# Opening phase in token pieces, sample tile joined for two column blocks, scores of the samples in four column groups

## What is computed

```
h = rmsnorm(x, norm_g)
z = h @ w_in                                   # (tokens, 4096) @ (4096, 9728)
u_a, gate_a, glu_val, glu_gate, gate_b, q, gate_c = split(z)
o_a = pool_mix(u_a) * silu(gate_a)             # windowed means 2/4/8/16 minus token, group map, scale
a   = glu_val * sigmoid(glu_gate)
o_b = (silu(layernorm(depthwise_conv31(a))) @ w_pw) * silu(gate_b)
o_c = softmax(q @ mem_k.T / 16) @ mem_v * silu(gate_c)    # 4 heads, 256 memory tokens
y   = rmsnorm(x + concat(o_a, o_b, o_c) @ w_out, final_norm_g)
```

## Time and profile before

| | us |
|---|---|
| median of 3 runs | 1980.24 (1979.48 to 1980.29) |
| profiled execution | 1981.93 |
| its span, slowest core (core 4) | 1980.4 |
| spans of the eight cores | 1962.9 to 1980.4 |
| TensorE busy | 1853.8 (94%) |
| VectorE busy | 971.4 (49%) |
| ScalarE busy | 357.1 (18%) |
| Pool busy | 142.0 (7%) |

### The profile page before, as it was taken

One profiled execution on the slowest core, in us unless ns is written; L12 is line 12 of the kernel. 1 busy time (PEld: TensorE's weight loads), 2 busy tenths in 40 slices (PEclk: granted clock), 3 DMA queues, 4 the chain that ended last, 5 costly groups with the idle time before them and its releaser, 6 DMA issues.

```text
span 1980.4 us, 29544 instructions; the slowest of 8 cores (1962.9 to 1980.4 us)
## 1 busy us (share of the span) xinstructions
PE 1853.8 (94%) x11388; PEld 941.7 (48%) x11592; DVE 971.4 (49%) x1367; ACT 357.1 (18%) x626; POOL 142.0 (7%) x270
## 2 busy tenths in 40 slices
PE   2768999899999999999999999999989999999997
PEld 1435555555444544544445555554444444444443
DVE  4548898848888888898580111121000110000355
ACT  4531011011011111011141232321000111111222
POOL 0000010110000000000001111100010000000000
PEclk9989999999999999999999999999999999999999
DMA  8854977695535444445446999745469577556897
GB/s 231 245 130 77 169 131 128 112 170 100 92 67 90 91 80 76 87 80 100 69 61 94 154 147 151 117 70 99 86 106 188 172 154 157 115 130 146 220 302 240
DMA packets 82091, 259.20 MB, mean 131 GB/s; under 512 B 12224, under 2 KB 18496, under 8 KB 76352
## 3 DMA queue, kind: packets, MB, share of 16 engines
q0 software_dynamic: 39328, 153.76, 48.6%
q1 hardware_dynamic: 42624, 103.53, 16.9%
HBM read 370.56 MB, written 40.45 MB: 208 GB/s over the span
## 4 chain that ended last, share of the span: by engine, by line
PE 88%; DMA 5%; DVE 3%; issue 2%; ACT 1%; DVEq 0%; SPq 0%; ACTq 0%; POOLq 0%
PE pz L364 77%; PE ps L364 10%; DMA slot<-w_in 2%; DVE HT L444 2%; DMA wo<-w_out 1%; ACT XN L425 1%; DMA XT<-x 1%; DMA slot<-w_mem_v 1%; PE ps L442 0%; DVE SQ L376 0%; DVE YB L497 0%; PE pz L442 0%; DVE CCA L386 0%; DVE HM L444 0%; ACT XN L420 0%
## 5 line engine op out<-in xcount | busy, mean ns | idle before, releaser
L364 PE MATMUL pz<-HT,slot 128*128 128x512 bf16 x4715 | 1132.6, 382 | 17.6 <-DMA slot<-w_in 3.9
L386 DVE SCALAR_TENSOR_TENSOR YB<-EA,CS,YB 128x512 f32<-128x512 f32 x720 | 480.5, 745 | 0.0
L364 PEld LDWEIGHTS pz<-HT,slot 128*128 128x128 bf16 x4864 | 331.3, 98 | 311.1 <-issue 21.2
L364 PE MATMUL ps<-HT,slot 128*128 128x64 bf16 (+1 forms) x2432 | 469.4, 199 | 5.1 <-ACT SGt L370 3.6
L364 PEld LDWEIGHTS ps<-HT,slot 128*128 128x128 bf16 x2432 | 233.6, 98 | 287.2 <-issue 13.5
L376 DVE TENSOR_TENSOR YT<-pz,XR 128x512 f32<-128x512 f32 (+1 forms) x54 | 37.3, 691 | 283.9 <-PE pz L364 236.6
L340 POOL DMA_DIRECT2D slot<-w_in x152 | 80.8, 533 | 1004.4 <-PE ps L364 757.6
L364 PE MATMUL pz<-wo,CCA 128*128 128x512 bf16 (+1 forms) x636 | 148.9, 382 | 1.7 <-ACT SGC L370 0.8
L364 PE MATMUL pz<-wo,CCB 128*128 128x512 bf16 (+1 forms) x635 | 147.7, 379 | 0.7
L370 ACT ACT_TABLE_LOAD x45 | 57.7, 1283 | 477.0 <-PE ps L364 245.1
L1000 ACT ACTIVATE JK<-YT 128x512 bf16<-128x512 f32 (+1 forms) x72 | 45.3, 630 | 436.7 <-DVE YT L376 436.7
(11 more groups left out here) (148 smaller groups left out, 1190.9 us busy)
## 6 DMA issues: line engine op xcount, KB each, us to landing
slot<-w_in POOLq DMA_DIRECT2D x152, 512.0 KB, 6.2
wo<-w_out POOLq DMA_DIRECT2D x32, 1024.0 KB, 18.4
XT<-x SPq DMA_DIRECT2D x8, 2048.0 KB, 13.8
XR<-x SPq DMA_DIRECT2D x64, 256.0 KB, 8.1
y<-YT SPq DMA_DIRECT2D x64, 256.0 KB, 8.2
YF<-y SPq DMA_DIRECT2D x24, 512.0 KB, 6.6
y<-YF SPq DMA_DIRECT2D x24, 512.0 KB, 9.3
slot<-w_mem_k POOLq DMA_DIRECT2D x16, 512.0 KB, 9.1
```

The source lines that it names most:

```text
L364: S.op("pe", lambda e: e.matmul(out, lhsT=lhsT, rhs=rhs, start=start, stop=stop), r=r, w=w, t=max(64, n) / 2400 + 0.0025)
L386: S.op("dve", lambda e: e.scalar_tensor_tensor(out=out, in0=a, scalar=s, in1=b, op0=op0, op1=op1), r=r, w=w, wa=wa, t=n / 960 + 0.13)
```

## The change

Three parts.

1. The opening. There are three XT and three XN buffers and, for this phase, two more weight slots. The order of the tiles is 8 (halo and samples), 0, 1, ..., 7, 9, 10. Tile 8's load is the first DMA of all; the next waits for the constants, the one after for tile 8's landing. The weight loads are let in two slots at a time by `w_gate`, behind the landing of a named tile. The first units are cut into pieces of 96, 256 and 128 tokens placed between the transposes, and they are GG0, V0 and GG1; unit V1 follows, and only then the two memory tiles. The evacuations of the small tokens and the main ones are split (`gg_small`, `gg_main`, `v_small`, `v_main`).
2. `qk_sample` takes the four samples of a group in turn for each chunk, so that neighbouring matmuls write different groups of 32 partitions, and gives its slots back at the end. The samples' steps are in rounds 1, 4, 7, 10 and their values in rounds 3, 6, 9, 11.
3. In the output's first six blocks the sample tile is computed once for two blocks: before an odd block's tiles, 64 matmuls alternate between the partitions 0 to 63 (block before) and 64 to 127 (this block).

```diff
-        XT = [at("XT", R, [D], F32), at("XT", R + 16384, [D], F32)]
+        XT = [at("XT", R, [D], F32), at("XT", R + 16384, [D], F32), at("XT", R_YB + 5 * 4352, [D], F32)]
...
-        for i, oo in enumerate((R_YB + 4352, R_YB + 3 * 4352)):
+        for i, oo in enumerate((R_YB + 4352, R_YB + 3 * 4352, R_AT + 5440)):
...
+        slots += [at("slot", R_AT + 13632 + 4096 * i, [2048], BF16) for i in range(2)]
...
-        free_slots = collections.deque(range(NSLOT))
+        free_slots = collections.deque((0, 1, 2, 3, NSLOT, NSLOT + 1, 4, 5))
...
-            while free_slots and wst["issue"] < len(loads):
+            while free_slots and wst["issue"] < min(len(loads), wst["limit"]):
...
+        ORD = (8, 0, 1, 2, 3, 4, 5, 6, 7, 9, 10)
...
+        def norm_load(n):
+            if n < 11:
+                src, rows = TILES[ORD[n]]
+                S.dma("sp", lambda e: e.dma_start(out=XT[n % 3][0][0:rows, :], in_=src), w=[XT[n % 3][1]])
...
+            norm_load(n + 3)
...
+        def w_gate(n, upto):
+            S.deps("pool", [XT[n % 3][1]], [])
+            wst["limit"] = upto
+            w_fill()
+
+        norm_load(0)
+        S.dma("sp", lambda e: e.dma_start(out=CS[:], in_=cs_d), w=[CSb])
...
+        S.deps("sp", [CSb], [])
+        norm_load(1)
+        S.deps("sp", [XT[0][1]], [])
+        norm_load(2)
+        FIRST = (U_GG, U_V, U_GG + 1)
...
+            for kc in range(32):
+                sl = fs[u][kc // 16]
+                view = slots[sl][0][:, :].rearrange("p (k n) -> p k n", k=16)
+                mm(out, view[:, kc % 16, :], HT[:, kc, a:b], kc == 0, kc == 31, [slots[sl][1]] + HTb[a // 128:(b + 127) // 128], [tb])
+            return k
...
+        whole(0)
+        esa_load(0)
+        whole(1)
+        w_gate(2, 2)
+        whole(2)
+        norm_scale(3)
+        norm_transpose(3, (0, 1))
+        w_gate(4, 4)
+        piece(0, 0, 256)
+        norm_transpose(3, (2, 3))
+        gg_small(0, piece(0, NPR, NT))
+        norm_scale(4)
+        norm_transpose(4, range(4))
+        piece(0, 256, 512)
+        w_gate(6, 6)
+        piece(1, 0, 256)
+        piece(1, 256, 512)
+        v_small(0, piece(1, NPR, NT))
+        whole(5)
+        whole(6)
+        piece(0, 512, 768)
+        piece(1, 512, 768)
+        w_gate(8, 8)
+        gg_small(1, piece(2, NPR, NT))
+        piece(2, 0, 256)
+        norm_scale(7)
+        norm_transpose(7, (0, 1))
+        piece(2, 256, 512)
+        norm_transpose(7, (2, 3))
+        piece(2, 512, 768)
+        norm_scale(8)
+        norm_transpose(8, (0, 1))
+        piece(0, 768, 896)
+        norm_transpose(8, (2, 3))
+        piece(1, 768, 896)
+        piece(2, 768, 896)
+        wst["limit"] = 1 << 30
+        for u in range(3):
+            piece(u, 896, 1024)
...
-        S.t["dve"] = S.t["pe"]
+        S.t["dve"] = S.t["pe"] + 7.0
...
-        al = collections.deque(a_units[1:])
+        run_unit("vv", 1)
+        for n in (9, 10):
+            norm_scale(n)
+            norm_transpose(n, range(4))
+        al = collections.deque(a_units)
...
-            for jj in range(4):
-                s_ = 4 * q + jj
-                w0 = NPR + (4 * s_ if s_ < 8 else 4 * s_ - 28)
-                sl = w_get("ck", s_)
...
+            got = [w_get("ck", 4 * q + jj) for jj in range(4)]
+            for h in range(4):
+                for ec in range(2):
+                    c = 2 * h + ec
+                    for jj in range(4):
...
-        steps = [(qk_sample, tr_sample, q) for q in range(4)] + [(qk_prompt, tr_prompt, ti) for ti in range(8)]
+        steps = []
+        for j in range(12):
+            steps.append((qk_sample, tr_sample, j // 3) if j % 3 == 1 else (qk_prompt, tr_prompt, j - (j + 1) // 3))
...
-            if 4 <= j < 8:
-                pv_sample(j - 4)
+            if j in (3, 6, 9, 11):
+                pv_sample((j - 1) // 3)
...
-        order = [(blk, ti) for blk in range(NBLK - NLAST) for ti in range(9)]
+        order = []
+        for blk in range(NBLK - NLAST):
+            if blk % 2:
+                order.append((blk, 9))
+            order += [(blk, ti) for ti in range(8)]
...
+        def pair_tile(n, blk, o_, ob):
+            for q in range(4):
+                for k in range(8):
+                    kc = 8 * q + k
+                    for h in range(2):
+                        t, tb = wo_list[4 * (blk - 1 + h) + q]
+                        mm(o_[64 * h:64 * h + 64, :], CC[kc][0][:, NPR:W], t[:, k, :], kc == 0, kc == 31, [tb, CC[kc][1]], [ob])
+                wo_release(4 * (blk - 1) + q)
+            yt, yb = YT[n % 4]
+            tt(yt[:], o_, XR[n % 4][0][:], ALU.add, [ob, XR[n % 4][1]], [yb], 512)
...
-                if not last and ti == 8:
+                if not last and ti == 7 and blk % 2:
                     wo_release(4 * blk + q)
```

More of the change, by code:

```diff
@@ L428, in norm_scale, with norm_transpose @@
                                                   scalar2=None, op0=ALU.mult), r=[xtb, nb], w=[xnb[1]], t=2.2)
-        def norm_transpose(i, rows, gcol, dst, dstb, c0, small):
-            b = i % 2
-            for q in range(4):
-                if small:
+            norm_load(n + 3)
+        def norm_transpose(n, qs):
+            i, rows = ORD[n], TILES[ORD[n]][1]
+            xn, xnb = XN[(n + n // 9) % 3], XNb[(n + n // 9) % 3]
+            if i < 9:
+                gcol, dst, dstb, c0 = C_G, HT, HTb[i], 128 * i
+            else:
+                gcol, dst, dstb, c0 = C_MG, HM, HMb[i - 9], (i - 9) * 128
+            for q in qs:
+                if i < 9:
                     k = ps()
@@ L502, in v_evac @@
             bg.append(("conv%d" % j, conv_gen(j)))
+        def v_evac(j, zi, si):
+            v_small(j, si)
+            v_main(j, zi)
         def sq_half(j, h):
@@ L685, in build_program @@
[L685 to L694 removed]
+        def w_gate(n, upto):
[4 more added lines that the diff above has]
+        S.dma("sp", lambda e: e.dma_start(out=CS[:], in_=cs_d), w=[CSb])
+        S.dma("sp", lambda e: e.dma_start(out=IDF[:], in_=id_d), w=[IDFb])
@@ new lines, in build_program, with piece @@
+        S.op("dve", lambda e: e.tensor_copy(out=IDB[:], in_=IDF[:]), r=[IDFb], w=[IDb])
+        S.deps("sp", [CSb], [])
[3 more added lines that the diff above has]
+        FIRST = (U_GG, U_V, U_GG + 1)
+        fs = {}
+        rot["pz"] = 3
+        def piece(u, a, b):
+            if u not in fs:
+                fs[u] = [w_get("in", 2 * FIRST[u] + h) for h in range(2)]
+            if b == NT:
+                k = ps()
+                out, tb = PS[k][:, 0:NT - a], PSb[k]
+            else:
+                k = None
+                out, tb = PZ[u][:, a:b], PZb[u]
+            for kc in range(32):
[3 more added lines that the diff above has]
+            return k
@@ new lines, in whole @@
+        def whole(n):
+            norm_scale(n)
[16 more added lines that the diff above has]
+        piece(1, 0, 256)
@@ L696, in build_program @@
+        piece(1, 768, 896)
[3 more added lines that the diff above has]
+            piece(u, 896, 1024)
+            for sl in fs[u]:
+                w_release(sl)
+            if u == 0:
+                gg_main(0, 0)
+            elif u == 1:
+                v_main(0, 1)
+            else:
+                gg_main(1, 2)
+        wp_load(0)
+        eus_load(0)
+        S.t["dve"] = S.t["pe"] + 7.0
         a_units = [(k, 3 * g + i) for g in range(4) for k in ("u", "ga") for i in range(3)]
@@ L920, in wo_release @@
         def wo_release(k):
-            if k not in (1, 2) and (wo_list[k] is not WO[0] or len(wo_list) < 20):
+            if k not in (1, 2) and (wo_list[k] is not WO[0] or len(wo_list) < 24):
                 wo_free.append(wo_list[k])
@@ L986, in build_program @@
             xr_load()
-            if n == (NBLK - NLAST) * 9:
+            if blk == NBLK - NLAST and ti == 0:
                 for _ in range(6):
@@ L990, in build_program @@
             o_, ob = PO[n % 8]
+            if ti == 9:
+                pair_tile(n, blk, o_, ob)
+                continue
+            t0, x0, rows = OT[ti]
+            last = blk >= NBLK - NLAST
             for q in range(4):
```

130 lines of the change are left out of this document (47 added, 83 removed).

## The result

| | before | after |
|---|---|---|
| median, us | 1980.24 (1979.48 to 1980.29) | 2004.56 (2002.68 to 2009.42, 4 runs) |
| ratio | | 1.0128, 95% interval 1.0105 to 1.0151 |
| profiled execution, its span | 1981.93, 1980.4 | 2002.68, 2001.4 |
| TensorE busy in the profile (the one before lacks 204 of 11592 matmul records) | 1853.8 | 1846.5 |
| start of the first memory unit (k unit), cores 0 / 4 / 7 | 176.5 / 173.6 / 174.5 | 190.4 / 188.9 / 191.6 |

What follows compares the result with a forecast made beforehand. TensorE was taken as the bound in the output, standing still for long only in the first 158.4 us. From 1981.9, +8 - 22 - 5.4 - 2.5 gave 1960.0; the median, 1.7 lower, 1958 us, range [1943, 1975], forecast's chance 0.58.

Steps and rivals of the forecast that it cites:

- Opening, +8: Up to the first memory unit: 181.8 us after against 173.6 before, 8 us lost, bounds -6 and +12.
- three waits that I found in the queues: Opening: TensorE idle 9.6, 2.9 and 6.1 us before tiles 4, 5 and 7, behind small evacuations on ScalarE and VectorE.
- Middle, 0: Between opening and scores: order changes of the plan cost 0 us, bounds -5 and +5.
- 31 us of cover: Middle: VectorE's last normalisation ends at 1039.9, its first matmul starts at 1071.2; only delay beyond 31 us counts.
- Scores, -5.4: Sample scores: four column groups in turn take 0.9 us for 2.24, four times, 5.4 us saved, bounds -5.4 and +4.9.
- Slots, -2.5: Around the sample scores: most of 3.9 us of waits for w_in slots go, 2.5 us saved, bounds -5.8 and +2.
- Output, -22: Output: three pair tiles take 22.0 us in place of six sample tiles' 44.0, 22 us saved, bounds -22 and +19.
- B: Column groups overlap only in part: pair tile 9.4 us, scores gain nothing, 1970 us; chance 0.12.
- C: Column groups don't overlap: pair tile 14.2 us, scores 3.46 in place of 2.24, 1989 us, slower; chance 0.08.
- D: No overlap and each weight load bare: pair tile 20.9 us, scores 7.0, 2023 us; chance 0.04.
- Rival A: Opening is level or better, -6 in place of +8, giving 1944 us; chance 0.18.
- the third buffer gains nothing: Opening: after the second tile no step waits for a tile's transfer, so the added buffer gains nothing.

Runs made afterwards that it cites:

- e7: Changed kernel with the scaling of tiles 4, 5 and 7 put ahead of the small evacuations; ratio 1.0046 to the kernel before.
- e5: Changed kernel with the planner's estimate of VectorE's time set back to TensorE's after the memory tiles; ratio 1.0070 to the kernel before.
- e6: Changed kernel with four KST buffers (from which memory keys and values are stored) in place of two; ratio 1.0069 to the kernel before.
- e12: Changed kernel with due convolution steps and their squares issued ahead of a memory unit's copies; ratio 1.0053 to the kernel before.
- e2: Kernel before with only the sample scores in column groups and the new order of steps; ratio 0.9990 to the kernel before.
- e1: Kernel before with only the pair tiles of the output; ratio 0.9904 to the kernel before.
- e8: Changed kernel with the weight slots handed out from another start (2, 3, 4, 5 first); ratio 1.0087 to the kernel before.
- e11: Kernel before, so the old opening, with both the grouped scores and the pair tiles; ratio 0.9868 to the kernel before.
- e3: Kernel before with only the new opening; ratio 1.0206 to the kernel before.
- e9: Changed kernel with the edits of e5, e6, e7 and e8 together; no ratio, spans of cores 0 to 3 1951.4, 1961.8, 1947.2, 1958.3 us.

## Why the prediction was wrong, point by point

- **Opening, +8: 13.9, 15.3 and 17.1 on cores 0, 4 and 7.** The mechanism was right, step by step, and two terms of the sum were too small. Tile 1's transposes started at 27.6 for 25.2: ScalarE waited 2.47 us for its load, which had landed later than the pace that I assumed, and landing times were the one input without a row. The lower clock behind a pause was the other. I took 0.9 us for it per pause (a piece of 4.4 for 3.5), although in the earlier trace rows it already costs 2.3 (4.47 less 10 x 0.216). It cost 1.7 us in the first piece (5.19 for 3.46), 3.1 in the three behind tile 4 (13.45 for 10.4) and 2.2 in the two behind tile 6 (9.14 for 6.9); the granted clock is 0.78 in both of these stretches. (For the first piece, as for the earlier trace rows, the profile has the doubled times and shows no lowered granted clock.) The pauses themselves were right: 9.47 for 9.6 before tile 4. V1 began at 149.3 for 141.1 on core 0, and the gap behind it was 26.1 for 25.5. I had checked my steps against the old order, and trusted them to 4 us; the old order has long segments and so few pauses, and could not test what pauses cost. The bound of +12 was too near. The three waits that I found in the queues were worth 16 us (e7), just the idle time of their rows: 9.47 + 2.75 + 5.87, less the 2.08 that remain in e7.
- **Middle, 0: +22, +20 and +25 (23.2 in the mean of the eight cores), the step that failed most.** I asked whether VectorE's last normalisation would still be in time at 1071 us and found 31 us of cover. That is a cover at the end of the stretch. The loss arose between 310 and 361 us, where the new order brings memory units, a convolution's end and the pooling together: three queues, each strictly in order, wait on each other in a ring, and TensorE waits 14.48 us for its PSUM tile. I named ±5 for a changed plan because the stretch lost only 16 us before; what was lost before does not bound what a new order loses. e5 and e6 each move part of it; e12, which only issues the due convolution steps and their squares ahead of the copies, gives 18 of the 23 us back.
- **Scores, -5.4: about -5.0 in themselves** (four times 2.24 - 0.99), so the overlap was right. **Slots, -2.5: wrong in sign.** The waits for w_in rose from 0.9 to 3.5 us in the mean of the eight cores (3.2 in e2 alone) instead of vanishing. I had priced core 4, whose 3.9 us before are the exception: cores 0 and 7 had 0.4 and 0. Part two as a whole is worth 2 us with an interval that holds zero, 3.4 by the means of cores 0 to 3.
- **Output, -22: the pair tiles are worth 23** (3 x (14.68 - 7.03)), and e1 gives 19 (14 to 24). Rivals B, C and D fall with the 7.03 us. What I had not looked at is the start of the stage: the opening's new slot list turned which pair of slots the last units lie in, and the first w_out tiles wait for those slots. It cost 8 us (e8). The prediction's sentence that only weight loads stand behind each gate was true of the queue, and missed that slot numbers run on through the whole kernel.
- **Sum.** The measured terms on core 0: +13.9 opening, +22.0 middle, +0.2 to the first output product, -7.9 output, +28.2 in all (1973.2 to 2001.4). For the two parts that cut work the forecast's terms come to -29.9, and e11 gives -26 (-37 to -15); for the part that orders it they come to +8, and e3 gives +41. So the sum failed most at its term 0 for the middle, then at the size of the opening's +8 and at the start of the output, to which it gave no term. Rival A, the opening level or better, holds once the queues are put right (e7: level), and the claim that the third buffer gains nothing was not tried by itself.

What is left of the middle: the stretch from first memory unit to first LNX product is 5 us above the kernel before in e12 (mean of eight cores) and 10 in e9 (cores 0 to 3). On core 0 the wait lists name it: TensorE's waits for SGt are 9.1 and 9.3 us for 5.4, those for weight loads 9.1 and 11.0 for 6.0. What it would take to bring them back was not tried. Whether fewer DMA transfers around 310 to 320 us would help (share 1.04 from 300 to 350 us in the changed kernel) was not tried.

## What to carry to other kernels

When work is reordered, write down for each in-order engine what stands behind every instruction that may wait, also far from the edit: a small evacuation ahead of a scaling cost 16 us here, and a square behind a memory unit's copy some 15. Resources that are handed out in turn (slots, buffers) carry a rotation made at the start through to the end, so check who gets which one at the next stage. Slack at the end of a stretch covers no pause in its middle, and savings of work (pair tiles, column groups) can be taken without the reordering that came with them.

## What the runs showed of the hardware

Column groups of one array, taken in turn, run side by side almost in full, weight loads included. Two groups of 64 columns take 64 matmuls of 512 columns in 7.03 us, 0.110 us each, where one alone needs 0.216: 1.96 of the ideal 2. Four groups of 32 columns take 32 matmuls of 256 in 0.99 us, 0.031 each, where one alone would need 0.108 (an estimate, half of 0.216): 3.5 of the ideal 4. With eight matmuls in a row per group the same 32 took 2.24 us. The loads overlap each other too. In the changed kernel 72 of them cover 3.8 us:

```profile
L367 PEld LDWEIGHTS pz<-wo,CCA 128*64 128x64 bf16 x72 | 3.8, 110 | 4.3 <-issue 1.3
```

In the earlier trace rows, with one group, they cover 7.4 us at the same 0.110 us each. The Trainium skill ("TensorE: Matmul & The Clock Gate", Part 3) lets a weight load overlap only with another row group; all of these use the same rows, and the measurement decides against it for this form (by its 2.38x for three column groups the prediction estimated 9.1 us for a pair tile). What the prediction cites of the fast weight load stands in the tiling page of the Trainium skill under "Restrictions", not under Performance Considerations.
